# Splitting the last raw weight chunks of linear attention, one wider mask matmul, input loads moved into the first feed-forward, and identity matmuls at the end of tails

## The reference

```python
x = layer_norm(ALPHA * x + gate * 0.5 * swiglu(modulate(x)))        # for the latent tokens, layer 0 also for the context
h = modulate(x)
y = window_sink_attention(h, h_ctx)                                 # layer 0: band |q-k| <= 128, context keys, a sink per head
y = real(fft2(h)) @ w_o                                             # layer 1
x = layer_norm(ALPHA * x + gate * y); x = another half feed-forward
```

## Time and profile before

| | |
|---|---|
| median of three runs | 2187.61 us (2186.68 to 2189.37) |
| the profiled execution's own time | 2184.68 us |
| its span | 2182.7 us |
| PE, DVE, ACT busy | 2103.3, 1617.4, 972.5 us |
| granted TensorE clock, mean | 0.993 of 2.4 GHz |
| weight loads | 407 of 1 MB, median 5.0 us from issue to landing |

### The profile page before, as it was taken

The page is one execution under the profiler, slowest core; times in us unless marked ns, Lnnn a source line. Parts: engine busy times, 40 slices in busy tenths (PEclk is TensorE's granted clock), DMA queues, the critical chain, the costliest instruction groups (busy, mean ns, idle before and its releaser), DMA issues. The chain is left out here.

```text
span 2182.7 us, 37144 instructions
## 1 busy us (share of the span) xinstructions
PE 2103.3 (96%) x15744; PEld 1874.4 (86%) x15744; DVE 1617.4 (74%) x2326; ACT 972.5 (45%) x1345; POOL 2.3 (0%) x8
## 2 busy tenths in 40 slices
PE   7999999999999999999999799989999999999998
PEld 5899999887899999977999689889799986768886
DVE  3887877777787788775887778676787776667556
ACT  3434534427543454344434466344454454215443
POOL 0000000000000000000000000000000000000000
PEclk9999999999999999999999999999999999999999
DMA  9866688430689768733988211300388822305541
GB/s 394 331 240 248 235 313 337 155 116 1 248 350 360 298 274 323 309 134 145 366 327 307 67 59 59 136 23 3 126 333 349 339 98 78 116 31 210 209 177 39
DMA packets 65812, 450.83 MB, mean 207 GB/s; under 512 B 7959, under 2 KB 9240, under 8 KB 12696
## 3 DMA queue, kind: packets, MB, share of 16 engines
q1 hardware_dynamic: 65688, 449.11, 53.4%
HBM read 448.03 MB, written 1.05 MB: 206 GB/s over the span
## 5 line engine op out<-in xcount | busy, mean ns | idle before, releaser
L541 PEld LDWEIGHTS banks<-ffn_h_split,ffn_weights_split 128*128 128x128 f32 x6336 | 769.6, 192 | 13.4 <-DVE ffn_weights_split L632 4.7
L541 PE MATMUL banks<-ffn_h_split,ffn_weights_split 128*128 128x256 f32 x6336 | 773.6, 284 | 7.3 <-DVE ffn_h_split L653 6.0
L826 DVE TENSOR_TENSOR ffn_weights_split<-weight_ring,ffn_weights_split 128x2048 fp32r<-128x2048 f32 x223 | 510.4, 2289 | 222.2 <-ACT ffn_weights_split L715 222.2
L715 ACT CAST ffn_weights_split<-weight_ring 128x2048 fp32r<-128x2048 f32 x223 | 424.0, 1901 | 162.7 <-PE banks L559 153.1
L559 PE MATMUL banks<-ffn_weights_split,ffn_hidden_split 128*128 128x512 f32 x1512 | 356.8, 392 | 2.4 <-DVE ffn_hidden_split L752 2.4
L559 PEld LDWEIGHTS banks<-ffn_weights_split,ffn_hidden_split 128*128 128x128 f32 x1512 | 280.9, 189 | 59.2 <-DVE ffn_hidden_split L752 2.8
L782 DVE CUSTOM_DVE_ANT_0 weight_ring<-weight_ring,first_arena,cols 128x1024 f32<-128x1024 f32 x196 | 240.5, 1280 | 0.4 <-ACT first_arena L725 0.4
L679 ACT ACTIVATE ffn_arena<-banks 128x256 f32<-128x256 f32 x132 | 50.6, 383 | 417.3 <-PE banks L541 417.3
L514 PE MATMUL banks<-ffn_h_split,ffn_weights_split 128*128 128x512 f32 x352 | 124.7, 399 | 0.2 <-DVE ffn_h_split L653 0.2
L516 PE MATMUL banks<-ffn_h_split,ffn_weights_split 128*128 128x256 f32 x352 | 98.7, 280 | 0.0
L121 ACT CAST weight_ring_split<-weight_ring 128x2048 fp32r<-128x2048 f32 x34 | 64.5, 1905 | 56.1 <-DMA weight_ring<-in_weights 38.4
(11 more groups left out here) (414 smaller groups left out, 2632.2 us busy)
## 6 DMA issues: line engine op xcount, KB each, us to landing
weight_ring<-in_weights SPq DMA_DIRECT2D x407, 1024.0 KB, 5.0
first_arena<-in_norm_rows SPq DMA_DIRECT2D x12, 512.0 KB, 7.2
first_arena<-in_c_rows SPq DMA_DIRECT2D x4, 512.0 KB, 11.9
first_arena<-in_ctx_rows SPq DMA_DIRECT2D x2, 1024.0 KB
h<-in_ctx SPq DMA_DIRECT2D x1, 1024.0 KB, 17.2
side<-in_x SPq DMA_DIRECT2D x1, 1024.0 KB
x<-in_x_rows SPq DMA_DIRECT2D x1, 1024.0 KB
hyena_tables<-in_hy_filt SPq DMA_DIRECT2D x1, 1024.0 KB
```

Of the source, the lines that this page charges most:

```text
L541: last = nc.tensor.matmul(bank[:, half * T:half * T + T], w[:, x, sl], hs[:, k, y, :], start=(k == 0 and x + y == 0), stop=(k == DT - 1 an ...
L715: nc.scalar.copy(wsplit[:, c % S, 0, :], raw).then_inc(self.split_hi.sem, 1)
L826: nc.vector.tensor_tensor(wsplit[:, c % S, 1, :], core.wbuf[:, (self.first + at(c)) % NSLOT, :], wsplit[:, c % S, 0, :].bitcast(F32), ALU. ...
```

## The change

- `Tail.pe`: after the context rows are turned, PE waits for the first step of the tail on DVE and multiplies the identity by itself 68 times into bank 0, before it waits for the context to be scaled. At the end of every live tail behind which nothing follows in its block, but for the context's own, it does so 14 times into bank 3. Four tails are of this kind: ahead of attention, Fourier, the recurrent mixer and Hyena.
- `Opening`: `later` holds x alone. The rows and the tables are loaded in the first (context) feed-forward, behind its chunk of place 20, and DVE waits for them ahead of that feed-forward's tail.
- Attention: the mask is kept whole (256 columns), ACT rounds it and the identity to float32r between its copies for `v` and `q1`, and one float32r matmul of 256 columns for each bank takes the place of the float32 one of 128.
- `ab`: `lg0`, `lg1`, `gz0` and `gz1` are split, with four more copies in ACT's order and four more subtractions in DVE's; `lg` lands in the upper half of h, and `gz` is copied out only behind `gz1`. The stage takes 27 slots for 23. Of the two early chunks of the output projection that were split at its end only the first stays there; ACT's copy of the second moves to `gdn_scan`, and its subtraction goes to POOL there.

The diff, cut:

```diff
--- before.py
+++ after.py
@@ -266,6 +266,8 @@
             self.context.pe_turn(pe)
+            pe.wait_ge(self.steps.sem, self.steps.base + 1)
+            self.pe_warm(core.ps[0][:, 0:P], 68)
             pe.wait_ge(self.context.done.sem, self.context.done.base + DT)
@@ -287,6 +289,8 @@
             self.pe_warm(core.ps[3][:, 0:P], 8)
+        elif self.turn_at:
+            self.pe_warm(core.ps[3][:, 0:P], 14)
@@ -457,7 +461,7 @@
     def __init__(self, core, h, f, tail, sides=None, refresh=None, modulate=None, vector=None, before=None,
-                 opening=None, split_next=False, ahead=(), wide=False):
+                 opening=None, split_next=False, ahead=(), needs_ahead=False, wide=False):
         self.wide, self.opening, self.split_next, self.ahead = wide, opening, split_next, ahead
@@ -470,6 +474,8 @@
         self.copied, self.summed = take("attn_exp", FFT if wide else 0), take("attn_p_ready", FFT if wide else 0)
+        self.ahead_loaded = take("inputs_loaded_ahead", 16 * len(ahead) if needs_ahead else 0)
+        self.needs_ahead = needs_ahead
         self.modulated = take("ffn_modulated", DT + 1 if modulate else 0)
@@ -843,6 +849,8 @@
         dve.wait_ge(used.sem, self.first + slots.total())
+        if self.needs_ahead:
+            dve.wait_ge(self.ahead_loaded.sem, self.ahead_loaded.base + 16 * len(self.ahead))
         tail.dve_coefficients(dve)
@@ -874,6 +882,9 @@
         self.core.low(dve, self.core.nc.vector, self.first + 2 * half, self.w_low)
+
+    def pool_weight(self, pool, half):
+        self.core.low(pool, self.core.nc.gpsimd, self.first + 2 * half, self.w_low)
@@ -1224,7 +1235,7 @@
     pv_done, o_copied = take("attn_pv_done", N), take("attn_o_copied", DT)
-    dsteps = take("dve_steps", 4 * N)
+    dsteps, mask_split = take("dve_steps", 4 * N), take("cleared", 1)
     SCORES = ((0, 1), (6, 7))
@@ -1252,9 +1263,8 @@
                                          kk[lo:lo + 64, s, t // 4, :], start=(s == 0), stop=False, skip_group_check=True)
-                far = (1 - b) * P
                 for e in range(2):
-                    last = nc.tensor.matmul(core.ps[banks[e]][:, far:far + P], core.ident[:, :], a["mask"][:, b, :],
+                    last = nc.tensor.matmul(core.ps[banks[e]][:, 0:T], a["ident_r"], a["mask_r"][:, b, :],
                                             start=False, stop=True, skip_group_check=True)
@@ -1337,6 +1347,7 @@
             pe.wait_ge(roped.sem, roped.base + 9)
+            pe.wait_ge(mask_split.sem, mask_split.base + 1)
             scores(0)
@@ -1464,6 +1475,8 @@
             high("v")
+            nc.scalar.copy(a["ident_r"], core.ident)
+            nc.scalar.copy(a["mask_r"], a["mask"]).then_inc(mask_split.sem, 1)
             high("q1")
@@ -1623,8 +1636,8 @@
 ENTRY = {"lq": 0, "lk": 1, "gk0": 3, "gk1": 5, "lv0": 7, "lv1": 9, "gv0": 11, "gv1": 13,
-         "gq0": 15, "gq1": 17, "lg0": 19, "lg1": 20, "gz0": 21, "gz1": 22}
-SPLIT = ("lk", "gk0", "gk1", "lv0", "lv1", "gv0", "gv1", "gq0", "gq1")
+         "gq0": 15, "gq1": 17, "lg0": 19, "lg1": 21, "gz0": 23, "gz1": 25}
+SPLIT = ("lk", "gk0", "gk1", "lv0", "lv1", "gv0", "gv1", "gq0", "gq1", "lg0", "lg1", "gz0", "gz1")
 LOW = {c: i + 1 for i, c in enumerate(SPLIT)}
@@ -1885,17 +1898,17 @@
             keys(2), keys(3)
-            raw("lg0")
+            latent("lg0")
             step(5)
-            raw("lg1")
+            latent("lg1")
             step(6)
...
                 turn(f"v{t}", [place(4 + hd, t) for hd in range(NG)])
-            raw("gz0")
+            latent("gz0")
             step(7)
-            raw("gz1")
+            latent("gz1")
             pe.wait_ge(state.sem, state.base + 16)
@@ -2042,32 +2055,36 @@
             silu(16, 12)
+            high("lg0")
             act.wait_ge(convd.sem, convd.base + 12)
...
             silu(6, 15)
+            high("lg1")
             side_out("key0", tm(b["ktm"], 0), flat)
...
             silu(18, 16)
+            high("gz0")
             side_out("key2", tm(b["ktm"], 2), flat)
...
             silu(8, 18)
-            last_out("lg0", "lg0", b["lg"][:, 0:2, :])
+            last_out("lg0", "lg0", b["lg_raw"][:, 0:2, :])
             silu(10, 20)
+            high("gz1")
             act.wait_ge(silud.sem, silud.base + 10)
             square(4), square(5)
-            last_out("lg1", "lg1", b["lg"][:, 2:4, :])
+            last_out("lg1", "lg1", b["lg_raw"][:, 2:4, :])
             norm(4), norm(5)
...
             for hd in range(NG):
-                nc.scalar.activation(b["lg"][:, hd, :], b["lg"][:, hd, :], ACT.Silu).then_inc(mact.sem, 1)
-            early.act_weight(act, 0), early.act_weight(act, 1)
-            last_out("gz0", "gz0", b["gz"][:, 0:2, :])
+                nc.scalar.activation(b["lg_raw"][:, hd, :], b["lg_raw"][:, hd, :], ACT.Silu).then_inc(mact.sem, 1)
+            early.act_weight(act, 0)
             act.wait_ge(kv.sem, kv.base + 16)
...
                 nc.scalar.activation(b["msq"][:, hd, :], o_of(hd), ACT.Square).then_inc(msquared.sem, 1)
+            last_out("gz0", "gz1", b["gz"][:, 0:2, :])
             last_out("gz1", "gz1", b["gz"][:, 2:4, :])
@@ -2216,21 +2233,25 @@
             scale(3)
+            low("lg0")
             query_conv("gq0", 0, 8)
             update(3)
+            low("lg1")
             query_conv("gq1", 1, 10)
...
             update(4)
+            low("gz0")
             update(5)
+            low("gz1")
             update(6)
...
             update(7)
-            early.dve_weight(dve, 0), early.dve_weight(dve, 1)
+            early.dve_weight(dve, 0)
             step, z = Steps(dve, msteps), b["lg"]
...
             for hd in range(NG):
-                last = nc.vector.scalar_tensor_tensor(z[:, hd, :], o_of(hd), core.col("gla_norm_w")[:, 0:1], z[:, hd, :],
+                last = nc.vector.scalar_tensor_tensor(z[:, hd, :], o_of(hd), core.col("gla_norm_w")[:, 0:1], b["lg_raw"][:, hd, :],
                                                       ALU.mult, ALU.mult)
@@ -2576,6 +2597,10 @@
             early.sp(sp)
+
+        @block.gpsimd
+        def _(pool):
+            early.pool_weight(pool, 1)
@@ -2636,6 +2661,7 @@
                     .then_inc(st_s[d].sem, 1)
+            early.act_weight(act, 1)
             nc.scalar.activation(gz[:, :, :], gz[:, :, :], ACT.Silu).then_inc(gate_s.sem, 1)
@@ -3085,8 +3111,8 @@
 PLAN = [8, ffn_plan(0), ffn_plan(1), 11, 4, 2, ffn_plan(2), ffn_plan(3), 4, 2, ffn_plan(4),
-        23, 4, 2, ffn_plan(5), 24, 4, 2, ffn_plan(6)]
-PAIRED = {3: range(2, 11, 2), 4: (1, 3), 8: (1, 3), 11: range(2, 19, 2), 12: (1, 3), 15: range(1, 24, 2), 16: (1, 3)}
+        27, 4, 2, ffn_plan(5), 24, 4, 2, ffn_plan(6)]
+PAIRED = {3: range(2, 11, 2), 4: (1, 3), 8: (1, 3), 11: range(2, 27, 2), 12: (1, 3), 15: range(1, 24, 2), 16: (1, 3)}
 SOURCE, _loads = [], 0
@@ -3206,7 +3232,7 @@
             table = top[0]
-            at = dict(mask=carve(TT, P), cos=carve(T), sin=carve(T), swap=carve(P), bv=carve(T), sink=carve(NH))
+            at = dict(mask=carve(TT, T), cos=carve(T), sin=carve(T), swap=carve(P), bv=carve(T), sink=carve(NH))
             top[0] = table
@@ -3219,16 +3245,19 @@
                                   [(cols[:, :], a["cols"]), (selector[:, :], a["selector"]), (consts[:, :, :], a["consts"])],
-                                  (hf[:, :, :], a["ctx"]), [(xm, a["x"]), (cx, a["ctx_rows"]), (x[:, :, :], a["x_rows"])] + tables)
+                                  (hf[:, :, :], a["ctx"]), [(xm, a["x"])])
                 tail = Tail(core, "ln", cx, vec(0, 2, 1), 0.5 / ALPHA, tail_space(spread, mix),
...
                 ctx_ffn = FeedForward(core, hf, f, tail, sides_of(0, crow), modulate=(xm, hf, vec(0, 1), vec(0, 0)),
-                                      opening=opening)
+                                      opening=opening, needs_ahead=True,
+                                      ahead=[(cx, a["ctx_rows"]), (x[:, :, :], a["x_rows"])] + tables)
                 tail = Tail(core, "ln", x, vec(0, 2), 0.5 / ALPHA, tail_space(spread, mix, rows),
...
             with phase("attention", 10320, False), nc.sbuf_tensor("attention_h_high", [P, DT, 2, T], F32R) as h_high, \
-                    nc.sbuf_tensor("attention_h_low", [P, DT, 2, T], F32R) as h_low:
+                    nc.sbuf_tensor("attention_h_low", [P, DT, 2, T], F32R) as h_low, \
+                    nc.sbuf_tensor("attention_mask", [P, P + TT * T], F32R) as mask_r:
+                at |= dict(ident_r=mask_r[:, 0:P], mask_r=mask_r[:, P:].rearrange("p (b t) -> p b t", b=TT))
                 at |= dict(q=carve(DT, T), k=carve(2, 2, T), v=carve(2, TT, T), sm=carve(4, 2, 2 * T), pt=carve(2, 2, 2 * T),
@@ -3278,7 +3307,7 @@
             hc = side
-            b = dict(qkv=carve(20, T), gz=y[:, 0:NG, :], lg=y[:, NG:2 * NG, :], g=carve(TK, 8), beta=carve(TK, 8),
+            b = dict(qkv=carve(20, T), gz=y[:, 0:NG, :], lg=y[:, NG:2 * NG, :], lg_raw=hf[:, NG:2 * NG, :], g=carve(TK, 8), beta=carve(TK, 8),
```

(2 more changed lines are left out.)

## The result

| | before | after |
|---|---|---|
| median (lowest to highest), 12 runs each | 2188.27 us (2185.23 to 2190.18) | 2191.87 us (2186.61 to 2195.98) |
| ratio after to before | | 1.0016, 95% interval 1.0009 to 1.0024 |
| profiled execution, its span | 2184.68 us, 2182.7 us | 2195.69 us, 2193.9 us |
| mean granted clock of it | 0.993 | 0.985 |

The change costs 3.6 us by the medians. The forecast was 2.0 us less than before; the measured time lies 1.4 us above the upper end of the range. The profiled execution of after is one of its longest, 3.8 us over its median, so its trace shows more of some losses than the median holds; a second one of the same kernel, further down, took 2188.24 us.

What follows compares the result with a forecast made beforehand. PE was taken as the bound, busy 2103.3 of 2182.7 us. The terms -4.0 - 2.9 + 2.1 + 5.3 - 2.5 + 0 = -2.0 us took 2187.6 to 2185.6 us, range 2179.0 to 2190.5.

Steps and rivals of the forecast that it cites:

- Part 1: First feed-forward: with fewer loads in `later`, PE's 2.36 us wait and 1.63 us of slow clock go, -4.0 us.
- The rival that the start stays as it is: First feed-forward: the pause at 65.7 is DVE's own, not the load's; sum +2.0, 2189.6 us; chance 0.12.
- Part 2: Attention loop: float32r mask matmul saves 0.21 us a round in 14 rounds, -2.9 us; bounds 0 and -3.4.
- Part 3: Fourteen identity matmuls behind tails: +1.7 us at attention, +0.2 each at Fourier and Hyena, +2.1 in all.
- Part 4: Recurrent mixer's tail: 68 identity matmuls outlast PE's pause by 6.4 us; +5.3 us including that tail's fourteen.
- The rival that the batches aren't on the path: Identity matmuls fit the pauses: recurrent batch -1.0 for +5.3, sum -8.3, 2179.3 us; chance 0.20.
- Part 5: Four chunks in `ab`: -5.0 us on PE, +2.0 wait ahead of step 4, +0.5 at the end, -2.5 us.
- Part 6: Subtraction moved to POOL in `gdn_scan`: costs 0 us; up to 4.6 us if the shared port lock alone holds.
- the third rival: POOL blocks DVE in `gdn_scan`: at the slow bound sum +11.4, 2199.0 us; chance 0.08.

Runs made afterwards that it cites:

- the sixty-eight alone: Only the 68 identity matmuls ahead of the recurrent mixer added to the kernel before: 2192.16 us, 3.3 more, ratio 1.0019.
- part 5 alone: Only the four split chunks in `ab` added to the kernel before, `lg0` split ahead of `update(3)`: 2188.77 us, 0.1 less, ratio 0.9999.
- the kernel with thirty-six: Changed kernel with `lg0` split moved, attention pauses filled, batches of 6 for 14 and 36 for 68: 2172.65 us, ratio 0.9933 to the kernel before.

## Why the prediction was wrong, point by point

**Part 1, right, in part by luck.** -4.0 forecast, -4.1 measured alone, -3.8 by the traces; no wait and no stretch at 1.2 GHz at 65 in any execution with it. The rival that the start stays as it is falls. But 1.63 of the 4.0 us were a fall of the clock read from one trace. It comes in 4 of 6 executions, and the wait itself is 1.70 to 2.48 us, so for the kernel before alone the gain is nearer to 3.4 us: the four executions that load the small mask there take 34.06 us on average for 30.7. The agreement to 0.1 us is closer than either number is known.

**Part 2, the step right, the sum too large.** The step of 0.21 us a round is as forecast: the lead over the kernel before grows by 0.20 to 0.21 in each of 12 rounds, not 14, which is 2.5 us. Against executions without a fall the loop is shorter by just this (99.22 us for 96.72 where the pauses are filled). What I left out is the pause ahead of `scores(2)`. With the shorter matmuls it grows from 1.67 to 2.08 us, and the clock fell behind it in 9 of 9 executions, where it was 4 of 6. That takes back 0.7 us on average, so -1.8 us by the traces and -1.3 measured alone, with an interval that reaches from -3.3 to +0.7. Whether the longer pause is why it falls more often isn't shown by 9 against 6 executions.

**Part 3, sized by the wrong clock, with a sum that comes out near.** The forecast has +2.1 for three of the tails, and its sum for the recurrent mixer holds 3.1 + 0.45 - 1.90 = 1.65 for the fourth, 3.75 us in all. Measured alone +4.9, with an interval from 3.5 to 7.9. The barrier's price was nearly right, +1.53 at each of the four for 1.65 to 1.7. The clock given back was mis-sized, in the step "these two come to +0.2 each, so in all +1.7 + 0.2 + 0.2 = +2.1". I took 1.5 us at Fourier from one trace as if it were always lost. When it is lost it is 1.7, but that is in 2 of 10 executions, 0.3 on average; at Hyena 1.1 come back on average, and not 1.5; and at attention, where I had none, a fall of 1.7 us came in 3 of 10. These errors have both signs: by the traces the part is +3.4 alone and +4.1 beside the sixty-eight, so its sum came out near, by luck, and its time doesn't tell the forecast from what happened.

**Part 4, right.** +5.3 with the fourteens' 1.65 in it, so +3.65; +3.5 by the traces and +3.3 measured alone. In the trace of the sixty-eight alone 6.26 us are added and 2.70 come back behind it. The rival that the batches aren't on the path falls, by this and by part 3.

**Part 5, the term that failed.** Its steps are there: PE saves 1.25 us a chunk, -5.0; step 4 waits 2.02 us for 2.0; the end of `ab` is 0.49 us later for 0.5 (PE's wait for DVE there is 1.30 us for 0.81). What failed is the choice "-2.5 us; with no wait -5.0, with a fall of the clock behind the wait, priced at 1.6 as in part 1, -0.9". The clock does fall, in 4 of 5 executions with the wait, and costs more than 1.6: in part 5 alone 1.75 us until the next chunk and 1.3 within it, 3.1 us; on average over the five, 2.2. And behind the end of `ab`, where the forecast counts 0.5 us of lateness and no clock, the falls become more: 9 of 9 executions with part 5 have one, 6 of 9 without, and from there to the scan PE takes 82.5 us and not 80.6, 2.0 more with the 0.5 in it (a rough size, since the nine without part 5 lie between 78.6 and 82.8). So -5.0 + 2.0 + 2.2 + 2.0 = +1.2 us, +1.1 by the unrounded numbers, for -2.5 forecast. The times agree within what they can tell: -0.1 measured alone (interval -2.2 to +1.5), +0.7 by taking it out. The move of one split, by which both the wait and the stretch behind it go, is worth 5.6 us on the changed kernel, and 4.8 by the traces.

**Part 6, right.** POOL takes 4.53 us, DVE's rows beside it are unchanged, and the stretch of PE that holds the scan takes 80.74 us with and without it, so the third rival falls. The estimate of 4.6 us that I took from the Trainium skill, GPSIMD Engine Reference, Engine selection, agrees with the row. Of the two rules in SBUF - State Buffer, Who interferes with whom, the row bears out the second: DVE, with one operand in a bank, was not kept waiting.

By the times the misses are -0.1 (start), +1.6 (mask), +1.1 (fourteens), -0.3 (sixty-eight) and +2.4 (part 5), 4.8 of the 5.6 us between -2.0 and +3.6. By the traces part 5 alone is +3.6 of them, the mask +1.1, and the rest under 0.5 each. None of the rivals is what happened: the forecast's waits and savings came as it says, and it had the clock wrong, at nothing behind the new wait and at the end of `ab`, and elsewhere by what one execution showed. The range was too narrow above, since its bound of -0.9 for part 5 was priced from a stretch of 1.6 us elsewhere.

## What to carry to other kernels

Read a fall of the clock out of several executions, not one: at one place it came back every time, at another in 2 of 10, and a batch of identity matmuls can earn only what is lost on average. Such a batch has to end before its pause does: 68 in a pause of 8.8 us cost 3.3 us, 36 shortened the tail by 2.5; 14 ahead of a barrier cost 1.53 us each, 6 delayed nothing and kept the clock at Hyena in both executions, where it had fallen in 10 of 10. And a short new wait on PE costs its own length and often a slow stretch behind it, here 2.0 and, in 4 of 5 executions, 1.6 to 3.1 us. So where a helper engine gets new work, put it behind what PE is waiting for.

## What the runs showed of the hardware that I had not expected

- The same pause, with the same work around it, is followed by 1.2 GHz in one execution and not in the next: 2.02 and 1.98 us ahead of step 4 in the changed kernel, granted clock 0.51 and 1.00 behind it; 1.67 and 1.66 us ahead of `scores(2)` in the kernel before, 1.00 and 0.50. Two executions of the changed kernel are 7.5 us apart, and most of it arises at such places: 3.1 us between step 4 and the next step, 2.6 between the end of `ab` and the scan, 1.7 in Hyena at 1823.
- The recorded clock isn't to be taken alone. In 10 of 18 executions it is 1.00 from 17 to 41 us, while 16 matmuls of 256 columns take 1.93 us there, as long as in the other eight at a recorded 0.50. In these eight such a group took 1.07 us just before, at the full clock.
- Filling pauses isn't shown to narrow the spread: the changed kernel's 12 runs lie within 9.4 us, the 5 with fitted batches within 5.0, but so do 12 runs of the kernel before.
- In the kernel with thirty-six, PE now waits 2.14 us for a load of `in_w_gate` behind the first projection of `ab`. The work ahead of it has become shorter than the load, which the longer pauses had hidden; this was not followed up.
